# Expert gate and up weights as four consecutive rows per partition, and tokens gathered by every fourth feature

## The reference

```
def hier_moe(x, w_grp, b_grp, w_rt, b_rt, w_gate, w_up, w_down):
    xt = x.reshape(b * t, d)                      # 512 tokens x 1024 features
    ... # softmax over 4 groups, best group, best 2 of its 4 experts, weights top_w
    gate = jnp.sum(jax.nn.one_hot(expert_id, 16) * top_w[..., None], axis=1)
    def step(acc, e_in):                          # 16 experts, hidden width 256
        wg, wu, wd, ge = e_in
        hdn = jax.nn.silu(xt @ wg) * (xt @ wu)
        return acc + ge[:, None] * (hdn @ wd), None
```

## Time and profile before

| | |
|---|---|
| time, median of 3 runs | 2709.46 us |
| lowest and highest | 2707.43 and 2716.48 us |
| profiled execution, first to last instruction (span) | 2711.5 us |
| profiled execution, device time of its own | not given beside the span |
| TensorE busy | 90% of the span |
| mean granted TensorE clock | 0.940 of full |

### The profile page before, as it was taken

How to read it: one execution, slowest core, us unless ns; L and a number is a source line. 1 busy time by engine, 2 the same in 40 slices (tenths; PEclk the granted TensorE clock), 3 DMA queues, 4 the chain that set the end, 5 groups by cost and what they waited for, 6 DMA issues and landing times. The chain is left out here.

```text
span 2711.5 us, 34303 instructions
## 1 busy us (share of the span) xinstructions
PE 2428.3 (90%) x13040; PEld 1903.7 (70%) x13040; DVE 1235.1 (46%) x2484; ACT 1026.9 (38%) x1730; POOL 827.4 (31%) x281
## 2 busy tenths in 40 slices
PE   6999998879956978997999399999999899999998
PEld 5888887767734865666777276767887767667886
DVE  3655542564444226866554544455122444363123
ACT  3444332145521115762554223453223424543222
POOL 2443442234331410011334122224444212224442
PEclk9999998889977978997999599999999999999999
DMA  5116111168851342122787341313322321314321
GB/s 131 47 55 233 32 47 63 48 232 278 279 190 54 94 131 82 42 63 95 252 279 261 118 138 47 98 63 109 124 93 84 110 73 47 113 63 143 100 69 70
DMA packets 255117, 315.26 MB, mean 116 GB/s; under 512 B 53088, under 2 KB 173232, under 8 KB 254976
## 3 DMA queue, kind: packets, MB, share of 16 engines
q1 hardware_dynamic: 252672, 304.94, 35.1%
q0 software_dynamic: 2304, 8.39, 0.8%
HBM read 277.50 MB, written 35.79 MB: 116 GB/s over the span
## 5 line engine op out<-in xcount | busy, mean ns | idle before, releaser
L159 POOL TENSOR_TENSOR branch_weights_wl<-branch_weights_wf,branch_weights_wh 128x2048 fp32r<-128x2048 f32 (+1 forms) x66 | 302.2, 4578 | 728.1 <-ACT branch_weights_wh L153 728.1
L153 ACT ACTIVATE branch_weights_wh<-branch_weights_wf 128x2048 fp32r<-128x2048 f32 (+1 forms) x66 | 124.7, 1890 | 209.0 <-PE merge_acc L201 92.8
L201 PE MATMUL bmid_acc<-xh,branch_weights_wh 128*128 128x512 f32 x320 | 148.7, 465 | 8.9 <-PEq L72 8.9
L201 PE MATMUL merge_acc<-xh,branch_weights_wh 128*128 128x512 f32 x384 | 151.5, 395 | 3.4 <-PEq L72 3.4
L523 POOL TENSOR_TENSOR in_weights_wl<-in_weights_wf,in_weights_wh 128x1024 fp32r<-128x1024 f32 x32 | 79.6, 2487 | 238.2 <-ACT in_weights_wh L519 220.1
L201 PE MATMUL merge_acc<-xl,branch_weights_wh 128*128 128x512 f32 x384 | 151.4, 394 | 0.0
L201 PE MATMUL merge_acc<-xh,branch_weights_wl 128*128 128x512 f32 x384 | 151.4, 394 | 0.0
L159 POOL TENSOR_TENSOR nsa_weights_wl<-nsa_weights_wf,nsa_weights_wh 128x2048 fp32r<-128x2048 f32 x13 | 59.7, 4593 | 278.3 <-ACT nsa_weights_wh L153 278.3
L201 PE MATMUL bmid_acc<-xl,branch_weights_wh 128*128 128x512 f32 x320 | 127.3, 398 | 0.0
L201 PE MATMUL bmid_acc<-xh,branch_weights_wl 128*128 128x512 f32 x320 | 127.2, 398 | 0.0
L1757 PE MATMUL exp_ps_y<-rt_wf,exp_ht 128*128 128x512 f32 x256 | 118.8, 608 | 3.8 <-ACT exp_ht L1801 3.8
(11 more groups left out here) (596 smaller groups left out, 6554.0 us busy)
## 6 DMA issues: line engine op xcount, KB each, us to landing
branch_weights_wf<-w_in SPq DMA_DIRECT2D x56, 1024.0 KB, 5.1
rt_wf<-moe_w_down SPq DMA_DIRECT2D x32, 1024.0 KB, 5.4
in_weights_wf<-gdn_w_in SPq DMA_DIRECT2D x64, 256.0 KB, 3.4
rt_wf<-moe_w_gate SPq DMA_DIRECT2D x32, 512.0 KB, 7.3
rt_wf<-moe_w_up SPq DMA_DIRECT2D x32, 512.0 KB, 8.2
moe_rows<-rt_y SPq DMA_DIRECT2D x64, 256.0 KB, 2.1
moe_rows<-gdn_z SPq DMA_DIRECT2D x2, 6144.0 KB, 27.8
merge_bwf<-w_branch SPq DMA_DIRECT2D x12, 1024.0 KB, 5.0
```

What stands on the lines that cost most here:

```text
L153: act.activation(self.h[u][:, :, 0:self.cols(b)], self.s.f[u][:, :, 0:self.cols(b)], ACT.Copy).then_inc(self.s.hi_ready, 1)
L159: pool.tensor_tensor(self.l[u][:, :, 0:self.cols(b)], self.s.f[u][:, :, 0:self.cols(b)], self.h[u][:, :, 0:self.cols(b)].bitcast(F32), ALU ...
L201: mm = pe.matmul(self.acc[:, s, 0:cols], lhs[:, P * s:P * s + P], rhs, start=(u == 0 and k == 0 and n == 0), stop=(u == 1 and k == HALF - ...
```

## The change

The gate and up weights get another layout in the same tiles, and the tokens are gathered to fit it. Partition p of unit u now holds the four consecutive rows 512u + 4p to 512u + 4p + 3 of gate, one behind the other, and then the same four rows of up. Group k of the product is row 4p + k of each partition, so the gather takes as its stationary operand every fourth feature, 512u + k, 512u + k + 4, and so on. The moving operand of the gate and up product is two runs of 256 columns, 1024 numbers apart, in place of one run of 512. The number of DMAs, of products and of their columns stays.

```
+    @staticmethod
+    def by_matrix(tile):
+        return tile[:].rearrange("p k n -> p (k n)").rearrange("p (c k n) -> p c k n", c=2, k=HALF)
+
+    @staticmethod
+    def features(u, k):
+        return slice(HALF * P * u + k, HALF * P * (u + 1), HALF)
+
     def load_in(self, sp, b, u, e):
-        for c, w in ((0, self.gate), (HID, self.up)):
+        for c, w in enumerate((self.gate, self.up)):
             src = w[bass.ds(e, 1), HALF * P * u:HALF * P * (u + 1), :]
-            sp.dma_start(self.f[b][u][:, :, c:c + HID],
-                         src.rearrange("a (k p) n -> p (a k) n", p=P)).then_inc(self.loaded[b][u], 16)
+            sp.dma_start(self.by_matrix(self.f[b][u])[:, c],
+                         src.rearrange("a (p k) n -> p (a k) n", k=HALF)).then_inc(self.loaded[b][u], 16)
...
                         for kk in (2 * part, 2 * part + 1):
-                            k = HALF * v + kk
                             for t in range(TT):
                                 mm = pe.matmul(dst[:, kk // 2, 2 * P * (kk % 2):2 * P * (kk % 2) + 2 * P],
-                                               src[:, t, P * k:P * k + P], pick[:, t, :],
+                                               src[:, t, ws.features(v, kk)], pick[:, t, :],
                                                start=(t == 0), stop=(t == TT - 1))
...
-                                mm = pe.matmul(ps_gu[:, 0, :], x[:, HALF * u + k, P * b:P * b + P], w[b][u][:, k, :],
+                                mm = pe.matmul(ps_gu[:, 0, :].rearrange("p (c n) -> p c n", c=2),
+                                               x[:, HALF * u + k, P * b:P * b + P], ws.by_matrix(w[b][u])[:, :, k, :],
                                                start=(u == 0 and k == 0 and m == 0),
                                                stop=(u == 1 and k == HALF - 1 and m == 2))
```

## The result

The changed kernel takes 2823.6 us, the median of four runs (2822.4 to 2825.5); the kernel before takes 2710.5 us beside it (2707.4 to 2716.5). The ratio is 1.041, with an interval of 1.040 to 1.043: 113 us slower, far outside the range of 2700 to 2728 us. The profiled execution took 2824.15 us with a span of 2822.2, which is 110.7 us over the 2711.5 of before.

The account below looks back on a forecast made before the run. The prediction took TensorE's instruction stream to bound the kernel. Loads 0, gate and up 0 and gather 0, added to the 2711.5 us span less 2.0 us, gave 2710 us, range 2700 to 2728 us.

Parts of the forecast that it names:

- What bounds the kernel: Expert stages: TensorE's own instruction stream sets the beat, 12.98 us a block; no stage hangs on DMAs.
- the loads: Gate and up weight DMAs: longer rows start nothing sooner, costed at 0, with -2 us as bound.
- landings under 8 us: Sign of being right: gate and up loads land within 8 us of issue, without effect on time.
- The reserve: For loads, data land 1.6 us before ScalarE reads; for the gather, its weight load is hidden by only 4 ns.
- The moving operand of gate and up: Two runs of 256 columns in 768 products: costed at 0, bounds -13 to +4 us.
- The stationary operand: Gather's 1024 weight loads, now reading every fourth number: costed at 0, bounds -4 to +101 us.
- the first: Reading for the gather's stepped load: 110 ns and 5 fixed, 115 ns, under 116; cost 0, at most 3 us.
- the ceiling: Limit on reading, taken from L2094's moving operand: a number not beside the one before comes every 0.86 ns.
- the other reading: Gather's stepped load needs 1.72 ns a column, 220 ns; gather goes from 116 to 220 ns, +101 us.
- Rival (b): Gather's weight load is doubled: +101 us, 2811 us; chance 0.17.
- Rival (c): Gather's stepped load and moving read get in each other's way: +14 us, 2724 us, or half; chance 0.21.
- (d): Faster, from the gather's 4 ns and part of gate and up's 17 ns: about 2700 us, 2692 at the utmost; chance 0.08.

Follow-up runs that it names:

- experiment 1: Kernel before with only the gather's stationary operand taking every fourth feature, old weight layout and 1 KB rows kept: 2824.9 us, ratio 1.041.
- 8: Kernel before, old layout with 1 KB rows, each gather summing one token tile in place of four: 2686.8 us, ratio 0.991.
- 9: Kernel before with gathers summing one token tile in place of four, new layout with 4 KB rows, tokens reordered once per stage: 2692.6 us, ratio 0.993.
- experiment 2: Changed kernel with tokens reordered once per stage, so the gather's stationary operand is contiguous again: 2719.0 us, ratio 1.0026 to the kernel before.
- Experiment 3: Change with two consecutive rows per partition in place of four: 2 KB rows, gather takes every second feature; 2714.7 us, ratio 1.0012 to the kernel before.
- Experiment 6: Kernel before with gate and up products reading their 512 moving weights at steps 1, 2, 3 and 4: 2847.9 us, once.
- 4: Kernel before with the gather's eight feature groups read at steps 1 to 8, one each: 2790.4 us, once.
- experiment 5: Kernel before with the gather's moving operand cut to 128 or 64 columns, weight load contiguous or at step four: 2826.7 us, once, only paces used.
- 7: Kernel before, gather moving 64 columns, weight loads varied: float32 at steps 1, 2, 4; displaced neighbours; 64 columns at steps 1, 2, 4, 8: 2798.1 us, once.

## Why the prediction was wrong, and where it was right

**What bounds the kernel, and the loads: right.** TensorE's stream is the beat, before and after (120.00 of 120.00). The fewer packets (205,965 in place of 255,117), the lower DMA share and the somewhat earlier landings changed no time. The 8.6 us of the earlier trace rows are the slowest among the loads into one of the buffers; over all gate and up loads of stage one the slowest took 9.1 us, and 8.8 in the changed kernel, so the forecast sign "landings under 8 us" did not hold. The reserve stood even so: 641.00 + 9.1 is 650.1 us, 1.1 before ScalarE's read at 651.21. Experiments 1 and 8 with 9 show it from two sides.

**The moving operand of gate and up: right.** Two runs of 256 columns cost nothing: the products start 233 ns apart before and after, and experiment 2 keeps them at a period of 12.98 us.

**The reserve: right.** Only 4 ns lay between the gather's pace and the load's floor. Experiment 3 confirms that small excesses are paid in full: some 4 ns on 32 products is 0.13, and the period grew by 0.11 us.

**The stationary operand: the step that failed.** "I take the first, because a contiguous load already goes at only 0.83 ns a column, the very pace that the step forces on others". That was an argument by likeness: the pace of a moving operand was taken for the ceiling of a load, though no row showed a load with a step. The term was set at 0 to 3 ns a product and measured 116.4 (116.9 to 233.3), and the range left out the other reading altogether. Experiment 6 shows that the ceiling exists on the moving side; experiments 4, 5 and 7 show that a load has another, 1.82 ns for each 16-byte piece, or 233 ns for the 128 pieces of a step of four.

**Rival (b)** is what happened, at a chance of 0.17 and a price of +101 us. Its 104 ns per product came from the 1.72 ns a column of L2094; the runs show 116.4. It also left out the products at the half clock, which lost 20 ns each. With these, 976 x 0.1164 and 48 x 0.020 are 114.6 us; 26 of the 28 periods give back some 0.10 us of it each, 2.7 in all, where the first two gather products start 120 ns apart in place of 233, and the clock in the last period of stage one gives 1.7, which leaves 110.2 of the 110.7. Its signs held: records near 300 ns (329), a period of 16.3 us (16.61), a DMA share near 0.68 (0.59 to 0.62; it left out that longer rows lower the share too: experiment 1, with the old rows, has 0.65 and 0.67).

**Rival (c)**, the clash of two reads, is excluded by experiment 5, and **(d)** by the unchanged 233 ns of gate and up.

**The rule on 16-byte lines.** "Advanced Engine Details and Errata" of the Trainium skill, section "Memory Cachelines", wants at least two hits on a line. For the weight load the traces bear it out: 120 ns at two hits, 233 at one. For a rounded moving operand they don't: at two hits a line it takes 445 ns where it took 233. Of the two readings of the rule that I weighed, the one that doubles whatever is read at one hit was right for the load.

**Still open** is why a load pays 1.82 ns for each piece where the moving side gets a number every 0.87 ns, what spreads steps 5 to 8 over 220 to 240 ns, whether a piece is 16 bytes or four numbers (no run loads numbers of two bytes), and where some 20 of the 233 ns of a gate and up product go.

## What to carry to other kernels

Read the stationary operand of a product as carefully as the moving one: with 256 moving columns a weight load is hidden by a few nanoseconds only, and once TensorE never idles, each nanosecond beyond them is paid by every product. If a layout needs a permutation, pay for it once per tensor, or, for the stationary operand, choose one that uses at least two numbers of each 16 bytes; and see first whether the layout buys anything, which longer rows don't where no engine waits for a load. Where two readings of a limit differ by 100 us and no row shows the case, a likeness to another operand decides nothing: the range has to hold both.

## What the runs showed of the hardware that I had not expected

- A weight load takes the longer of 0.83 ns a column plus 5 ns and 1.82 ns per 16-byte piece that it touches: 112 ns contiguous, 120 at a step of two, 176 at three, 233 at four. The price of a piece doesn't depend on the clock (233 ns at both levels), that of a column does (112 and 213 ns contiguous). Float32 and rounded operands are alike, and so are 64, 128 and 256 moving columns.
- The moving operand obeys another rule: 233 ns for 512 neighbours, 445 at a step of two, 461 at four.
- A step of four in what a float32 copy on ScalarE reads nearly doubles it (four of 128 x 1024: 3.90 to 7.73 us), and writing with jumps of 128 numbers gives 7.25; eight subtractions on VectorE go from 4.90 to 7.98 and 7.82 us.
- Rows of 4 KB in place of 1 KB lower the DMA engines' share from 0.93 to 0.84 at 306 to 308 GB/s.
